# Experts in items of 160 slots: 32 slots multiplied with raw fp32 weights on four column tiles

## The reference, cut to what matters

```python
def moe_swiglu(h, router, w_gate, w_up, w_down):
    ...
    probs = jax.nn.softmax((ht @ router).astype(F32), axis=-1)
    top_p, top_i = lax.top_k(probs, TOP_K)
    top_p = top_p / jnp.sum(top_p, axis=-1, keepdims=True)
    ...
    for e in range(N_EXPERTS):
        out = out + gates[:, e:e + 1] * swiglu(ht, w_gate[e], w_up[e], w_down[e])
```

## Time and profile before

| | before |
|---|---|
| median of 3 runs | 3207.73 us |
| the profiled execution, its own time | 3206.4 us |
| its span | 3204.5 us |
| PE, DVE, ACT busy | 2784.8, 1747.1, 1349.8 us |
| mean granted TensorE clock | 0.935 |

### The profile page before, as it was taken

The page is one execution under the profiler, slowest core; times in us unless marked ns, Lnnn a source line. Parts: engine busy times, 40 slices in busy tenths (PEclk is TensorE's granted clock), DMA queues, the critical chain, the costliest instruction groups (busy, mean ns, idle before and its releaser), DMA issues. The chain is left out here.

```text
span 3204.5 us, 48703 instructions
## 1 busy us (share of the span) xinstructions
PE 2784.8 (87%) x19227; PEld 2188.4 (68%) x19227; DVE 1747.1 (55%) x2057; ACT 1349.8 (42%) x1560; POOL 260.9 (8%) x323
## 2 busy tenths in 40 slices
PE   6999699998999778998999988936759978799998
PEld 5776578886767546777777766615748767578886
DVE  4646444342746437888888873356343444445462
ACT  3543332222554326677777763352122242333232
POOL 4022010001104000000000001001100010010000
PEclk8999899999999889999999999968879989999999
DMA  3200234232200119999999984100022232334231
GB/s 118 69 2 3 78 94 111 79 107 68 89 20 3 53 47 321 341 331 353 342 340 349 340 323 117 43 7 2 3 66 77 76 101 63 79 92 112 78 104 48
DMA packets 392994, 404.49 MB, mean 126 GB/s; under 512 B 18090, under 2 KB 274438, under 8 KB 392838
## 3 DMA queue, kind: packets, MB, share of 16 engines
q1 hardware_dynamic: 389237, 389.14, 37.9%
q0 software_dynamic: 3600, 13.11, 1.1%
HBM read 391.73 MB, written 10.49 MB: 126 GB/s over the span
## 5 line engine op out<-in xcount | busy, mean ns | idle before, releaser
L2680 DVE TENSOR_TENSOR experts_w_lo<-experts_raw,experts_w_hi 128x2048 fp32r<-128x2048 f32 (+1 forms) x242 | 498.2, 2078 | 125.1 <-ACT experts_w_hi L2644 122.5
L2644 ACT ACTIVATE experts_w_hi<-experts_raw 128x2048 fp32r<-128x2048 f32 (+1 forms) x242 | 418.2, 1746 | 147.8 <-DMA experts_raw<-in_moe_gate 66.6
L2809 PE MATMUL experts_psum<-experts_w_hi,experts_xg_lo 128*128 128x512 f32 x576 | 236.9, 411 | 47.4 <-DVE experts_w_lo L2680 38.2
L2811 PE MATMUL experts_psum<-experts_w_hi,experts_xg_hi 128*128 128x512 f32 x576 | 231.9, 403 | 0.0
L2810 PE MATMUL experts_psum<-experts_w_lo,experts_xg_hi 128*128 128x512 f32 x576 | 231.1, 401 | 0.0
L1258 PE MATMUL proj_psum<-keep_act_hi,proj_w_lo 128*128 128x512 f32 x384 | 164.8, 429 | 33.6 <-DVE proj_w_lo L1228 33.6
L2809 PEld LDWEIGHTS experts_psum<-experts_w_hi,experts_xg_lo 128*128 128x128 f32 x576 | 110.9, 192 | 85.6 <-DVE experts_w_lo L2680 50.3
L1260 PE MATMUL proj_psum<-keep_act_hi,proj_w_hi 128*128 128x512 f32 x384 | 155.6, 405 | 0.0
L1259 PE MATMUL proj_psum<-keep_act_lo,proj_w_hi 128*128 128x512 f32 x384 | 154.5, 402 | 0.0
L588 PE MATMUL conv_ffn_psum<-keep_act_hi,conv_ffn_w_lo 128*128 128x512 f32 x352 | 142.2, 404 | 13.6 <-DVE conv_ffn_w_lo L551 13.6
L588 PE MATMUL ffn_psum<-keep_act_hi,ffn_w_lo 128*128 128x512 f32 x352 | 141.7, 403 | 12.5 <-DVE ffn_w_lo L551 12.5
(11 more groups left out here) (720 smaller groups left out, 6439.0 us busy)
## 6 DMA issues: line engine op xcount, KB each, us to landing
experts_raw<-in_moe_gate SPq DMA_DIRECT2D x74, 1024.0 KB
experts_raw<-in_moe_up SPq DMA_DIRECT2D x72, 1024.0 KB, 7.1
experts_raw<-in_moe_down SPq DMA_DIRECT2D x96, 768.0 KB, 5.7
conv_ffn_raw<-in_w_ffn_in SPq DMA_DIRECT2D x44, 512.0 KB, 5.0
proj_raw<-in_w_in SPq DMA_DIRECT2D x28, 768.0 KB, 4.4
ffn_raw<-in_ffn_gate SPq DMA_DIRECT2D x22, 512.0 KB, 4.0
ffn_raw<-in_ffn_up SPq DMA_DIRECT2D x22, 512.0 KB, 5.2
ffn_raw<-in_ffn_down SPq DMA_DIRECT2D x16, 704.0 KB, 5.8
```

The source lines that it names most:

```text
L2644: act.activation(w_hi[v % 2][:, s], raw[v % 2][:, s], ACT.Copy).then_inc(rounded, 1)
L2680: dve.tensor_tensor(w_lo[v % 2][:, s], raw[v % 2][:, s], w_hi[v % 2][:, s].bitcast(F32), ALU.subtract).then_inc(split, 1)
L2809: pe.matmul(out, lhs[1][:, first + k, :], w_hi[slot][:, cols], start=begin and k == 0, stop=False)
L2811: last = pe.matmul(out, lhs[0][:, first + k, :], w_hi[slot][:, cols], start=False, stop=end and k == kt - 1)
```

## The change

An item now has 160 slots. Slots 0 to 127 are computed as before. The 32 others (`QUAD`) go as true fp32, without splitting: their activations (`xo`, `ho`) are the stationary operand with 32 columns, the raw weights stream, 128 columns to each of four column tiles of the array, which write to partitions 0 to 31, 32 to 63, 64 to 95 and 96 to 127 of one bank. That is 4 matmuls for each k tile, 288 in an item, run after each unit's own matmuls (`rest_of_slots`). The result `h_o` or `y_o` is 128 x 128: (tile, slot) by column; it has its own Silu, multiplication, transpose, scaling, gather and two scatters in pieces of 128 columns. Since TensorE now reads the raw weights, a raw half is free only when it has done so (`raw_used`); the raw weights lie in a ring of five halves instead of two whole buffers, in place of the waits on `split`. The transposes of gathered rows write to banks 0, 1 and 3 instead of 4 and 5, and both halves of the first unit are loaded at once.

The diff, cut to its core (arguments, allocations and index arithmetic of the same kind are left out):

```diff
+QUAD = P // 4
+SLOTS = P + QUAD
+ITEMS = (2 * T + EXPERTS * (SLOTS - 1)) // SLOTS
 ITEM_COLS = 16
-def items_phase(m, prob, chosen, x_tok, x_rows, place, lists, table, slots, own_slot):
+PICKED = 2 * P
 ...
+        LIMITS = range(SLOTS, T, SLOTS)
+        ENDS = 17 + 2 * len(LIMITS) + 1
 ...
+            dve.wait_ge(counted, 5)
+            step(dve.tensor_copy(spare[:, 0:1], first_i[:, :]))
+            step(dve.tensor_scalar(spare[:, 1:2], spare[:, 0:1], float(P), None, ALU.add))
+            step(dve.tensor_scalar(piece[:, 0:1], spare[:, 0:1], float(QUAD), None, ALU.is_ge))
+            for q in (2, 3):
+                step(dve.scalar_tensor_tensor(out=piece[:, 0:1], in0=spare[:, 0:1], scalar=float(q * QUAD), in1=piece[:, 0:1],
+                                              op0=ALU.is_ge, op1=ALU.add))
+            step(dve.tensor_scalar(piece[:, 1:2], piece[:, 0:1], 4.0, None, ALU.add))
 ...
+            step(dve.tensor_copy(slots[:, 0:P], ints[:, :]))
+            step(dve.tensor_copy(slots[:, P:PICKED].rearrange("p (c n) -> p c n", c=4), more_ints[:, :, :]))
 ...
-        raw = [ph.sb(f"raw{s}", [P, SLOT_A]) for s in range(2)]
+        raw = [ph.sb(f"raw{s}", [P, SLOT_A // 2]) for s in range(RING)]
 ...
-                for q in parts:
-                    sp.wait_ge(split, i * (2 * U) + (2 * v + (2 if c < 2 else q + 1)))
+                for q in range(2):
+                    ring = (2 * v + q) % RING
+                    sp.wait_ge(raw_used, i * (2 * U) + (2 * v + q + 1))
 ...
-            load(0, 0, first, range(1))
-            sp.wait_ge(rows_landed, 16)
-            load(0, 0, first, range(1, 2))
+            load(0, 0, first)
+            sp.wait_ge(rows_landed, 2 * 16)
 ...
+                pool.wait_ge(xg_turned, n * 3 + 3)
                 pool.sem_inc(rows_asked, 1)
                 pool.indirect_dma_start(xg[:, :], None, x_rows[:, :], bass.IndirectOffsetOnAxis(ap=row_of_slot[:, 0:1], axis=0)
                                         ).then_inc(rows_landed, 16)
+                pool.indirect_dma_start(xg_o[:, :], None, x_rows[:, :], bass.IndirectOffsetOnAxis(ap=row_of_slot[0:QUAD, 1:2], axis=0)
+                                        ).then_inc(rows_landed, 16)
             def send(n):
+                pool.wait_ge(way_made, n + 1)
                 pool.wait_ge(y_kept_first, n + 2)
+                pool.sem_inc(y_asked, 1)
+                pool.indirect_dma_start(pieces, bass.IndirectOffsetOnAxis(ap=way_of_slot[:, 1:2], axis=0), y_o[:, 0, :], None
+                                        ).then_inc(y_landed, 16)
                 pool.wait_ge(y_kept_second, n + 2)
-                pool.wait_ge(way_made, n + 1)
                 pool.sem_inc(y_asked, 1)
                 pool.indirect_dma_start(y_rows[:, :], bass.IndirectOffsetOnAxis(ap=way_of_slot[:, 0:1], axis=0), y[:, :], None
                                         ).then_inc(y_landed, 16)
-                pool.wait_ge(y_landed, n * 16 + 16)
+                pool.indirect_dma_start(pieces, bass.IndirectOffsetOnAxis(ap=way_of_slot[:, 2:3], axis=0), y_o[:, 1, :], None
+                                        ).then_inc(y_landed, 16)
+                pool.wait_ge(y_landed, n * 48 + 48)
                 pool.sem_inc(y_free, 1)
 ...
                 if q == 0:
                     act.wait_ge(used, i * U + (v + 1))
                 s = slice(q * n, (q + 1) * n)
-                act.activation(w_hi[v % 2][:, s], raw[v % 2][:, s], ACT.Copy).then_inc(rounded, 1)
+                act.activation(w_hi[v % 2][:, s], raw[ring][:, 0:n], ACT.Copy).then_inc(rounded, 1)
 ...
+                act.wait_ge(xg_turned, n * 3 + 6)
+                act.activation(xo[:, :, :], turned_x(), ACT.Copy).then_inc(xg_done, 1)
 ...
-                        act.activation(h[:, :], ps[:, 0, :], ACT.Silu).then_inc(silu_done, 1)
+                        act.activation(h[:, :], ps[:, 0, :], ACT.Silu)
+                        act.wait_ge(raw_used, i * (2 * U) + (2 * v + 2 + RING))
+                        act.activation(h_o[:, :], ps[:, 4, 0:P], ACT.Silu).then_inc(silu_done, 1)
                     if v in (2, 4, 6):
                         j = v // 2 - 1
                         act.wait_ge(h_turned, i * PAIRS + (j + 2))
                         act.activation(ht_hi[:, 4 * j:4 * j + 4, :], four(2 + j % 2), ACT.Copy).then_inc(ht_rounded, 1)
+                        act.activation(ho[:, 4 * j:4 * j + 4, :], turned_o(), ACT.Copy).then_inc(ho_done, 1)
 ...
-                        act.activation(y[:, 0:BANK], ps[:, 6, :], ACT.Copy, scale=slot_weight[:, 0:1]).then_inc(y_kept_first, 1)
+                        act.activation(y[:, 0:BANK], ps[:, 6, :], ACT.Copy, scale=slot_weight[:, 0:1])
+                        act.wait_ge(raw_used, i * (2 * U) + (2 * (U - 2) + 2 + RING))
+                        act.activation(y_o[:, 0, :], ps[:, 4, 0:P], ACT.Copy, scale=slot_weight[:, 1:2]).then_inc(y_kept_first, 1)
 ...
-                        dve.tensor_tensor(h[:, :], h[:, :], ps[:, 1, :], ALU.mult).then_inc(h_done, 1)
+                        dve.tensor_tensor(h[:, :], h[:, :], ps[:, 1, :], ALU.mult)
+                        dve.wait_ge(raw_used, i * (2 * U) + (2 * v + 2 + RING))
+                        dve.tensor_tensor(h_o[:, :], h_o[:, :], ps[:, 5, 0:P], ALU.mult).then_inc(h_done, 1)
 ...
-                dve.tensor_scalar(y[:, BANK:D], ps[:, 7, :], slot_weight[:, 0:1], None, ALU.mult).then_inc(y_kept_second, 1)
+                dve.tensor_scalar(y[:, BANK:D], ps[:, 7, :], slot_weight[:, 0:1], None, ALU.mult)
+                dve.wait_ge(raw_used, i * (2 * U) + (2 * (U - 1) + 2 + RING))
+                dve.tensor_scalar(y_o[:, 1, :], ps[:, 5, 0:P], slot_weight[:, 1:2], None, ALU.mult).then_inc(y_kept_second, 1)
 ...
+                    pe.matmul(ps[:, 3, 0:3], pick[:, t, 0:P], lists[:, t, bass.ds(n, 1), :], start=t == 0, stop=t == TT - 1)
+                for t in range(TT):
+                    last = pe.matmul(ps[:, 3, 3:6], pick[:, t, P:PICKED], lists[:, t, bass.ds(n, 1), :], start=t == 0, stop=t == TT - 1)
                 last.then_inc(listed, 1)
 ...
+                for d in range(DT):
+                    last = pe.transpose(ps[:, 3, d * QUAD:(d + 1) * QUAD], xg_o[:, d * P:(d + 1) * P], m.ident[0:QUAD, 0:QUAD])
+                last.then_inc(xg_turned, 1)
 ...
+                    pe.transpose(ps[:, 5, 0:P], h_o[:, :], m.ident[:, :]).then_inc(h_turned, 1)
+                def rest_of_slots(v, x, first, begin, end):
+                    kt = DT if v < A else 6
+                    bank = 4 + (v % 2 if v < A else down_units[v - A][0])
+                    for k in range(kt):
+                        q, at = k // (kt // 2), k % (kt // 2) * BANK
+                        for c in range(4):
+                            last = pe.matmul(ps[c * QUAD:(c + 1) * QUAD, bank, 0:P], x[:, first + k, :],
+                                             raw[(2 * v + q) % RING][:, at + c * P:at + (c + 1) * P],
+                                             start=begin and k == 0, stop=end and k == kt - 1, skip_group_check=True)
+                        if at == (kt // 2 - 1) * BANK:
+                            last.then_inc(raw_used, 1)
 ...
+                    if v == 0:
+                        pe.wait_ge(y_kept_first, i + 1)
+                    if v == 1:
+                        pe.wait_ge(y_kept_second, i + 1)
+                    if v in (3, 5, 7):
+                        pe.wait_ge(ho_done, i * PAIRS + v // 2)
+                    if v == A:
+                        pe.wait_ge(silu_done, i * PAIRS + (PAIRS + 1))
+                    rest_of_slots(v, xo if v < A else ho, first, begin, end)
 ...
```

More of the change, by code:

```diff
@@ L2488, in _ @@
             step(dve.tensor_scalar(tiles[0:E, :], run[0:E, T - 1:T], 0.0, None, ALU.is_gt))
-            for q in range(1, TT):
-                step(dve.tensor_scalar(more[0:E, :], run[0:E, T - 1:T], float(q * P), None, ALU.is_gt))
+            for limit in LIMITS:
+                step(dve.tensor_scalar(more[0:E, :], run[0:E, T - 1:T], float(limit), None, ALU.is_gt))
                 step(dve.tensor_tensor(tiles[0:E, :], tiles[0:E, :], more[0:E, :], ALU.add))
@@ L2509, in _, with experts_phase @@
             step(dve.tensor_copy(table[0:1, N:N + 1], ps[0:1, 6, 0:1]))
-def experts_phase(m, x_rows, y_rows, place, lists, table, slots, own_slot):
+def experts_phase(m, x_rows, y_rows, place, lists, table, slots, spare, piece):
     nc = m.nc
@@ L2542, in experts_phase @@
         ps = ph.banks()
[L2543 to L2547, removed]
+        landed = [ph.sem(f"landed{s}") for s in range(RING)]
+        (rounded, split, used, raw_used, picked, listed, list_kept, rows_asked, xg_turned, xg_rounded, xg_done, weighed, way_step, way_made,
+         silu_done, h_done, h_turned, ht_rounded, ht_done, ho_done, y_kept_first, y_kept_second, y_asked, y_free, all_sent, tile_turned, tile_added) = (
```

(10 more changed lines are left out.)

110 lines of the change are left out of this document (58 added, 52 removed).

## The result

The kernel after takes 3111.89 us, the median of 4 runs (3109.25 to 3114.4), against 3205.64 us before, the median of 4 (the three runs of the start and one more). The ratio is 0.9707, with a 95% interval of 0.9691 to 0.9724: 93.7 us less. The forecast was 3142 us, between 3095 and 3278. The direction and the mechanism came out as forecast; the gain is 28 us larger.

The account below looks back on a forecast made before the run. The prediction took the weights' transfer as the bound, TensorE close behind. Items 2 to 8 -92.9, first item +20.0, edges +4.5 and +2.5 give -65.9 us: 3206.4 to 3140.5, median 1.3 higher, so 3142 us, range 3095 to 3278.

Parts of the forecast that it names:

- Fewer items: Expert phase: 8 items instead of 12, as no expert exceeds 160 tokens; 4 x 58.15 = 232.6 us go.
- Four tiles at once: fp32 part of an item: all four column tiles run together, 144 groups x 0.115 = 16.6 us an item.
- first rival: fp32 part: only two matmuls overlap, 33.1 us, +16.5 an item, 3274 us in all; chance 0.15.
- Switches: TensorE changing between 128 x 128 and column tiles, 20 times an item at 0.22 us: 4.4 us.
- Own and small work on PE: TensorE per item: 54.1 us busy as before, 2.5 for extra list records, transposes and gathered rows, 0.5 for the item's edge.
- The ring: Raw weight halves, now freed by TensorE: 12.6 us from release to use, 10.9 needed, so 1.7 us to spare.
- The edges: Before the first item and after the last: 4.5 us for tables, list and second gather, 2.5 for final scatters and scaling.
- The tables: Ahead of the first gather: 1.4 us for VectorE's added steps and iota, 1.9 us for the list's 8 more records.
- early load: Start of the expert phase: loading the first weights at once was set to zero, 3 us either way.
- The sum: Whole kernel: items 2 to 8 -92.9 us, first item +20.0, start and end +4.5 and +2.5; together -65.9 us.
- break-even: Expert phase: an item of 86.3 us would cancel the gain, 8.2 above the forecast item of 78.1 us.
- rival of two at a time: Same as the first rival: only two fp32 matmuls overlap, +132 us, 3274 us; chance 0.15.

Follow-up runs that it names:

- two counter-experiments: Kernel after with fp32 parts of neighbouring units paired (10 switches an item instead of 20): 3102.95 us; with each unit's fp32 part split in two (40 switches): 3130.75 us.

## Why the prediction was right, point by point

- *Fewer items, 232.6 us.* Right: 233 us with the four items taken away alone.
- *Four tiles at once, 16.6 us an item.* Right, by the row of the 64 x 64 tiles. At 0.109 us a group, 144 groups are 15.7 us. The rule on strict program order of the Trainium skill (TensorE: Matmul & The Clock Gate, Part 3, The mechanism) would have given the first rival, and the trace of before had already spoken against it; the runs do so too, within the look-ahead of three records a tile: the first records of tiles 1 to 3 start ahead of the second record of tile 0. Read strictly, the rule's half on weight loads in one row group would leave no overlap at all, and there is fourfold overlap.
- *Switches, 4.4 us.* The range held, the value was too high: 2.4 by the two counter-experiments, 3.3 by the trace. The row I took is an idle time of the weight load, not of the matmuls.
- *Own and small work on PE, 57.1 us with the item's edge.* Without switches and fp32 part 75.26 - 15.7 - 3.3 = 56.3 us. The 54.1 us were PE's busy time in one item of the kernel before, and I overlooked its clock. In that item TensorE stands idle for 1.75 us ahead of 1336.07, and then its granted clock is 0.50 for a while:

```profile
1337.40:1340.30 2.90, 2.90 (x8) 2.26 (x7) 2.73 (x7) 2.37 (x2) 0.00 (x0) 0.50 1.03 399
1337.78 0.63 PE L2809 MATMUL experts_psum<-experts_w_hi,experts_xg_lo 128*128 128x512 f32 x1
1338.21 0.63 PE L2810 MATMUL experts_psum<-experts_w_lo,experts_xg_hi 128*128 128x512 f32 x1
```

  Own matmuls start 0.43 us apart there, at 1.2 GHz, instead of 0.23. For seven of them that is 1.4 us of the 54.1, more than the 0.8 us by which the term was too large; in the item of the kernel after the clock is 1.00. How the rest divides between small work and the item's edge was not measured.
- *The ring fits with 1.7 us to spare.* Right for five halves (TensorE's matmuls wait 2.8 us for the split in seven items, its weight loads 9.3 us), but closer than I had it. The 1.75 and 2.08 us were means over halves of two sizes; a half of gate or up takes 1.9 and 2.3 us. With a unit of 7.7 us the chain has 0.9 + 7.7 + 2.8 = 11.4 us for 6.8 + 1.9 + 2.3 = 11.0, so a landing just above the median is late: 21 weight loads waited, up to 1.1 us. And with 52 of its 72 k tiles gone from the fp32 part, the item did not fall below 68.8 us.
- *The edges, +7 us.* This was the wrong term. The tables were right (3.2 of 3.3 us), but I set the early load to zero, "3 us either way", and it took 6 us off the way to the first matmul. In the kernel before, the second half of the weights landed late there, and `x_lo` waited on VectorE behind its split.
- *The sum* missed by 2.8 us in each of 8 items (0.9 streaming, 1.1 switches, 0.8 the rest) and 8 us at the edges: 30 us, as much as the median is below the forecast (3142 - 3111.9). All the terms erred to the same side, so none hid another. The break-even of 86.3 us an item was not near.

The range was wide upwards for the rival of two at a time. Tile by tile, where between one and two tiles run at once, the kernel takes 3255 us; the rival was priced at 3274.

One small reading of the prediction is off and changes nothing: the DMA digit is 9 in eight slices and 8 in the ninth.

## What to carry to other kernels

Work that is rounded up to whole passes over large weights can be cheaper as a small remainder in each pass, if the remainder fits on narrow array tiles that run side by side: here 32 slots cost 17 us in each of eight items, 138 us, where second passes for four experts had cost 58 us each, 233 us. With only two experts over 128 tokens the same numbers would make it a loss (an estimate: 138 against 116 us; not run). The order of the instructions decides whether such tiles overlap: put neighbours on different tiles, innermost. And when a later engine begins to read a buffer, its release moves; count the ring again for that (here one half more was worth 55 us).

## What the runs showed of the hardware that I had not expected

TensorE starts on a free column tile when three records are still to start on the tile before. The same 64 records took 1.95 us with four tiles in turn, 2.49 in runs of 16 records on two tiles, 4.33 in runs of 8 and 5.95 in runs of 16 on one tile. Four streams of fp32 from the same 128 partitions run at full pace: four records of 128 columns every 0.109 us, as often as a single tile starts one (0.109 us in the whole unit tile by tile). A change of form costs TensorE between 0.12 and 0.17 us.
